# Attention values held stationary, probabilities scaled on ScalarE ahead of their transposes, and a new order of the mixer units

## The reference

```python
u = rmsnorm(x, g_mix)
q, k, v, xb, yb = split(u @ w_in + b_in)
# attention: blocks of 128 queries, each with its own and the previous 128 keys
s = q @ k.T / 8 - slopes * dist                 # masked outside the window
m = max(max(s), sink);  p = exp(s - m)
p = p / (sum(p) + exp(sink - m));  attn = p @ v
# recurrence
xc = causal_conv4(xb)
a = exp(-8 * sigmoid(xc @ w_a) * softplus(-lam))
h[t] = a[t] * h[t-1] + sqrt(1 - a[t]**2) * (sigmoid(xc @ w_i) * xc)[t]
h_res = x + concat(attn, h * gelu(yb)) @ w_out + b_out
y = h_res + (silu(g) * up) @ w_ffn_out          # then a final rmsnorm
```

## Time and profile before

| | |
|---|---|
| time, three runs | 2332.24, 2332.38, 2334.09 us; median 2332.38 |
| span of the profiled execution (first to last instruction) | 2331.0 us |
| TensorE busy | 2251.5 us, 97% |
| VectorE busy | 1302.4 us, 56% |
| ScalarE busy | 878.1 us, 38% |
| granted TensorE clock, mean | 0.985 of full speed |
| bytes from HBM | 196.44 MB, 88 GB/s with the writes |

### The profile page before, as it was taken

How to read it: one execution, slowest core, us unless ns; L and a number is a source line. 1 busy time by engine, 2 the same in 40 slices (tenths; PEclk the granted TensorE clock), 3 DMA queues, 4 the chain that set the end, 5 groups by cost and what they waited for, 6 DMA issues and landing times.

```text
span 2331.0 us, 31209 instructions
## 1 busy us (share of the span) xinstructions
PE 2251.5 (97%) x12165; PEld 1915.8 (82%) x12165; DVE 1302.4 (56%) x2146; ACT 878.1 (38%) x1349; POOL 32.4 (1%) x66
## 2 busy tenths in 40 slices
PE   6999999999999999999999999999999899999996
PEld 6777888888777888888877788888888799999996
DVE  4786535356587544445668653545668665444453
ACT  4574223235375322223457432323446532222221
POOL 1000000000000000000000000000000000000000
PEclk9999999999999999999999999999999899999998
DMA  4123232323313233332322323233231122222221
GB/s 148 55 68 114 91 100 90 101 89 92 101 46 118 91 97 93 92 98 92 107 67 63 119 91 98 91 97 94 92 124 45 30 91 86 87 91 82 92 80 60
DMA packets 58586, 207.34 MB, mean 89 GB/s; under 512 B 7341, under 2 KB 7549, under 8 KB 58416
## 3 DMA queue, kind: packets, MB, share of 16 engines
q1 hardware_dynamic: 51840, 184.57, 25.5%
q0 software_dynamic: 3936, 12.03, 1.5%
q10 hardware_dynamic: 2656, 8.62, 1.0%
HBM read 196.44 MB, written 9.77 MB: 88 GB/s over the span
## 4 chain that ended last, share of the span: by engine, by line
PE 84%; DVE 9%; ACT 4%; issue 2%; DMA 1%; ACTq 0%; DVEq 0%; POOL 0%
PE bank L533 27%; PE bank L535 27%; PE bank L534 27%; DVE s_p L1258 2%; DVE w_lo L1157 1%; DVE xc L1297 1%; PE bank L661 1%; ACT s_p L961 1%; DVE om L1326 1%; PE bank L628 1%; DVE pT L1277 1%; PE bank L583 1%; ACT L986 0%; PE bank L557 0%; DVE ii L1325 0%
## 5 line engine op out<-in xcount | busy, mean ns | idle before, releaser
L533 PE MATMUL bank<-x_hi,w_hi 128*128 128x512 f32 (+1 forms) x2320 | 826.4, 356 | 3.7 <-DVE x_lo L1187 2.6
L535 PE MATMUL bank<-x_hi,w_lo 128*128 128x512 f32 (+1 forms) x2320 | 820.3, 354 | 0.0
L534 PE MATMUL bank<-x_lo,w_hi 128*128 128x512 f32 (+1 forms) x2320 | 819.5, 353 | 0.0
L883 ACT ACTIVATE w_hi<-w_raw 128x1024 fp32r<-128x1024 f32 (+1 forms) x360 | 374.1, 1040 | 1175.3 <-PE bank L535 1175.3
L533 PEld LDWEIGHTS bank<-x_hi,w_hi 128*128 128x128 f32 x2320 | 438.9, 189 | 79.8 <-issue 13.6
L1157 DVE TENSOR_TENSOR w_lo<-w_raw,w_hi 128x1024 fp32r<-128x1024 f32 (+1 forms) x360 | 431.8, 1200 | 127.7 <-ACT w_hi L883 125.9
L534 PEld LDWEIGHTS bank<-x_lo,w_hi 128*128 128x128 f32 x2320 | 439.1, 189 | 61.8 <-issue 1.4
L535 PEld LDWEIGHTS bank<-x_hi,w_lo 128*128 128x128 f32 x2320 | 438.3, 189 | 60.8
L533 PE MATMUL bank<-a_hi,w_hi 128*128 128x512 f32 (+1 forms) x1200 | 427.4, 356 | 6.2 <-DVE a_lo L1561 1.8
L535 PE MATMUL bank<-a_hi,w_lo 128*128 128x512 f32 (+1 forms) x1200 | 425.0, 354 | 0.0
L534 PE MATMUL bank<-a_lo,w_hi 128*128 128x512 f32 (+1 forms) x1200 | 424.3, 354 | 0.0
(11 more groups left out here) (240 smaller groups left out, 1475.0 us busy)
## 6 DMA issues: line engine op xcount, KB each, us to landing
w_raw<-in_units SPq DMA_DIRECT2D x296, 512.0 KB, 3.5
w_raw<-in_units SPq DMA_DIRECT2D x64, 448.0 KB, 3.3
x_tok<-in_x_prompt POOLq DMA_DIRECT2D x16, 512.0 KB, 6.1
out_y_p<-y_tok ACTq DMA_DIRECT2D x16, 512.0 KB, 3.0
gfin<-in_g_fin POOLq DMA_DIRECT2D x1, 512.0 KB, 7.1
kc_tok<-in_cache_k POOLq DMA_DIRECT2D x1, 512.0 KB, 6.9
vc_tok<-in_cache_v POOLq DMA_DIRECT2D x1, 512.0 KB, 7.3
out_nk_s<-in_cache_k POOLq DMA_DIRECT2D x1, 496.0 KB, 6.5
```

Source lines behind the costliest of these rows:

```text
L533: nc.tensor.matmul(out, h, hi[:, kt, c0:c1], start=(first and kt == kts[0]), stop=False)
L534: nc.tensor.matmul(out, h, lo[:, kt, c0:c1], start=False, stop=False)
L535: mm = nc.tensor.matmul(out, l, hi[:, kt, c0:c1], start=False, stop=(kt == kt_of[u] - 1))
L883: w_hi_ready.by(A(w_hi[:, u % RING, 0:n], w_raw[:, u % RAW, 0:n], ACT.Copy))
```

## The change

- `attend` takes the values as the stationary operand (128x64) and the transposed probabilities as the moving one (256 columns: both heads of a group). Group 0 writes partitions 0 to 63 of bank V, group 1 partitions 64 to 127, in turn for each half of the window: 4 matmuls. The result is transposed as it stands; `attn_out`, `attn_T`, `a_tok` and the first copy of `attn_hi` are gone, and `attn_hi` and `attn_lo` read bank V.
- The division by the sum moves ahead of the transposes: `normed`, four ScalarE copies with a scale for each unit, which wait for `rec_ready` from VectorE.
- TensorE's order becomes `scores(s)`, `attend(s-2)`, half of the projection unit, `gates` on odd s, the other half, `probs_T(s-1)`.
- ScalarE's order becomes `exps(s)`, `normed(s-1)`, `lru_root` (even s), `attn_hi` and `lru_gates` (odd s), the bias or the square, the copy of `probs_T(s-1)`, `gelu_tanh`, then as before. VectorE's copy of `probs_T(s-1)` moves behind `evacuate`, and `lru_scan` moves from behind `evacuate` to ahead of it.
- The channels of the attention output now lie in another order, so the 8 units of the output projection are loaded by 5 transfers each (one of half the unit, four of 64 KB) in place of one.

```diff
@@ load_unit (SyncE)
-                raw_in[u % RAW].by(sp.dma_start(w_raw[:, u % RAW, 0:n], units[u % NU, :, 0:n]))
+                raw, src, landed = w_raw[:, u % RAW, :], units[u % NU], raw_in[u % RAW]
+                if u % NU not in U_O:
+                    landed.by(sp.dma_start(raw[:, 0:n], src[:, 0:n]))
+                    return
+                landed.by(sp.dma_start(raw[:, JT * P:n], src[:, JT * P:n]))
+                for g in range(NKV):
+                    for c in range(2):
+                        k = 2 * g + c
+                        landed.by(sp.dma_start(
+                            raw[g * HEAD:(g + 1) * HEAD, 2 * c * P:2 * (c + 1) * P].rearrange("d (o m) -> d o m", o=2),
+                            src[:, k * P:(k + 1) * P].rearrange("(o d) m -> d o m", o=2)))
@@ mixers (TensorE)
 def probs_T(s):
-                    p_ready.wait(pe, b, s + 1)
+                    probs_ready.wait(pe, b, s + 1)
 def attend(s):
-                        attn_moved.wait(pe, b, qb)
-                    for hh in range(HH):
-                        g, jj = hh // 2, hh % 2
-                        head = g * JT + 2 * jp + jj
-                        for half in range(2):
-                            mm = nc.tensor.matmul(V[:, head * HEAD:(head + 1) * HEAD],
-                                                  pT[:, s % 2, 2 * hh + half, :],
-                                                  v_tok[:, qb + half, g * HEAD:(g + 1) * HEAD],
-                                                  start=(half == 0), stop=(half == 1))
+                        amix_ready.wait(pe, b, qb)
+                    for half in range(2):
+                        for g in range(NKV):
+                            d = slice(g * HEAD, (g + 1) * HEAD)
+                            mm = nc.tensor.matmul(V[d, 2 * jp * P:2 * (jp + 1) * P], v_tok[:, qb + half, d],
+                                                  pT[:, s % 2, 4 * g + half:4 * g + half + 3:2, :],
+                                                  start=(half == 0), stop=(half == 1), skip_group_check=True)
-                def attn_T(qb):
-                    atok_ready.wait(pe, b, qb + 1)
-                    for c in range(4):
-                        mm = nc.tensor.transpose(V[:, c * P:(c + 1) * P], a_tok[:, c * P:(c + 1) * P], ident[:, :])
-                    attnT_done.by(mm)
                 for s in range(NUN):
+                    scores(s)
+                    if s >= 2:
+                        attend(s - 2)
+                    if last:
+                        gemm(b, last, UH + s, x_hi, x_lo, None, None, 0)
+                    else:
+                        gemm(b, last, UH + s, x_hi, x_lo, None, list(range(KT // 2)))
+                    if s % 2 == 1:
+                        gates(s // 2)
+                    if last:
+                        gemm(b, last, UH + s, x_hi, x_lo, None, None, 1)
+                    else:
+                        gemm(b, last, UH + s, x_hi, x_lo, None, list(range(KT // 2, KT)))
                     if s >= 1:
                         probs_T(s - 1)
-                    if s >= 2:
-                        attend(s - 2)
-                    scores(s)
-                    gemm(b, last, UH + s, x_hi, x_lo)
-                    if s % 2 == 1:
-                        gates(s // 2)
-                    if s >= 3 and s % 2 == 1:
-                        attn_T((s - 3) // 2)
+                part(0, early)
+                attend(NUN - 2)
                 probs_T(NUN - 1)
-                attend(NUN - 2)
-                part(0, early)
+                part(1, early)
                 attend(NUN - 1)
-                part(1, early)
-                attn_T(QB - 1)
@@ mixers (ScalarE)
                 def attn_hi(qb):
-                    attnT_done.wait(act, b, qb + 1)
-                    attn_moved.by(A(a_tok[:, :], V[:, :], ACT.Copy))
-                    attn_moved.wait(act, b, qb + 1)
-                    amix_hi.by(A(a_hi[...], a_tok[...], ACT.Copy))
+                    av_done.wait(act, b, 2 * qb + 2)
+                    amix_hi.by(A(a_hi[...], V[...], ACT.Copy))
+                def normed(s):
+                    rec_ready.wait(act, b, s + 1)
+                    for hh in range(HH):
+                        head = hh // 2 * JT + 2 * (s % 2) + hh % 2
+                        ins = A(s_p[:, s % 2, hh, :], s_p[:, s % 2, hh, :], ACT.Copy,
+                                scale=rec[:, s // 2 % 2, head:head + 1])
+                    probs_ready.by(ins)
                 for s in range(NUN):
+                    exps(s)
                     if s >= 1:
-                        probs_T(s - 1)
-                    exps(s)
+                        normed(s - 1)
                     if s >= 2 and s % 2 == 0:
                         lru_root((s - 2) // 2)
+                    if s >= 3 and s % 2 == 1:
+                        attn_hi((s - 3) // 2)
+                    if s % 2 == 1:
+                        lru_gates(s // 2)
                    ...
-                        if c < LC - 1:
-                            gelu_tanh(c)
-                    if s >= 3 and s % 2 == 1:
-                        attn_hi((s - 3) // 2)
-                    if s % 2 == 1:
-                        lru_gates(s // 2)
+                    if s >= 1:
+                        probs_T(s - 1)
+                    if kind == "y" and c < LC - 1:
+                        gelu_tanh(c)
+                normed(NUN - 1)
                 probs_T(NUN - 1)
@@ mixers (VectorE)
                 for s in range(NUN):
-                    if s >= 1:
-                        probs_T(s - 1)
                     softmax_1(s)
                    ...
-                    if s >= 3 and s % 2 == 1:
-                        attn_out((s - 3) // 2)
                    ...
+                    if s >= 2 and s % 2 == 0:
+                        lru_scan((s - 2) // 2)
                    ...
+                    if s >= 1:
+                        probs_T(s - 1)
                    ...
-                    if s == NUN - 1:
-                        probs_T(s)
-                    if s >= 2 and s % 2 == 0:
-                        lru_scan((s - 2) // 2)
                     if kind == "y":
                         gelu_arg(c)
                 softmax_2(NUN - 1)
+                probs_T(NUN - 1)
```

More of the change, by code:

```diff
@@ L195, in hymba_layer @@
         h_prev = place("h_prev", [P, LC])
-        a_tok = place("a_tok", [P, NH * HEAD], at=[top[0]])
         ssum = place("ssum", [P, W])
@@ L282, in sem @@
             return ctx.enter_context(nc.semaphore(name))
-        raw_in = [Signal(sem(f"raw_in{i}"), NU // RAW, 16) for i in range(RAW)]
+        transfers = [1 + NKV * 2 if u in U_O else 1 for u in range(NU)]
+        raw_count = [sum(transfers[u % RAW:u + 1:RAW]) for u in range(NU)]
+        raw_in = [Signal(sem(f"raw_in{i}"), sum(transfers[i::RAW]), 16) for i in range(RAW)]
         w_hi_ready = Signal(sem("w_hi_ready"), NU)
@@ L320, in hymba_layer @@
         av_done = Signal(sem("av_done"), NUN)
-        atok_ready = Signal(sem("atok_ready"), QB)
-        attnT_done = Signal(sem("attnT_done"), QB)
-        attn_moved = Signal(sem("attn_moved"), QB)
+        rec_ready = Signal(sem("rec_ready"), NUN)
+        probs_ready = Signal(sem("probs_ready"), NUN)
         amix_hi = Signal(sem("amix_hi"), QB)
@@ L492, in _ @@
             for s in (gemm_done, xT_done, statx_done, stath_done, staty_done, vT_done, sc_done, pT_done,
-                      av_done, attnT_done,
+                      av_done,
                       gates_done, yT_done):
@@ L500, in smp_by, with gemm @@
                 ins.then_inc(smp_pe, 1)
[L502 to L508, removed]
+            def gemm(b, wide, u, hi, lo, tile_ready=None, kts=None, only=None, begins=0):
+                kts = kts or list(range(kt_of[u]))
+                first = kts[0] == begins
                 final = kts[-1] == kt_of[u] - 1
@@ L703, in part @@
                 def part(m, kts, c=0):
-                    gemm(b, last, U_O[m], a_hi, a_lo, mix_ready, kts, c)
+                    gemm(b, last, U_O[m], a_hi, a_lo, mix_ready, kts, c, KT - LC if kts else 0)
                 early, late, end_ = list(range(KT - LC, KT - 2)), [KT - 2] + list(range(KT - LC)), [KT - 1]
+                part(0, early)
+                attend(NUN - 2)
                 probs_T(NUN - 1)
-                attend(NUN - 2)
-                part(0, early)
+                part(1, early)
                 attend(NUN - 1)
-                part(1, early)
-                attn_T(QB - 1)
                 ahead = 2 if last else 3
@@ L860, in _ @@
             for s in (w_hi_ready, z_ready, sqx_ready, sqh_ready, sqy_ready, xhi_ready, hhi_ready, stdx_ready,
-                      stdh_ready, stdy_ready, p_ready, pTa_ready, attn_moved, amix_hi,
+                      stdh_ready, stdy_ready, p_ready, pTa_ready, probs_ready, amix_hi,
```

(24 more changed lines are left out.)

3 lines of the change are left out of this document (1 added, 2 removed).

## The result

The changed kernel takes 2419.45 us (median of 4 runs, 2415.77 to 2420.97) against 2332.31 for the kernel before: ratio 1.037, 95% interval 1.0355 to 1.0384. It is slower by 87 us; forecast was 2404, range 2368 to 2426.

A forecast was written before the change was run, and what follows sets the result against it. The prediction took the order of steps on three nearly full engines, a loop mostly through VectorE, as the bound. Blocks +59.6 and clock +12 made 72 on the 2331.0 span: 2403, 2404 us as time, range 2368 to 2426.

The forecast's parts named there:

- The loop: Durations added along the engines' new written orders for a steady mixer pair: 26.16 us against 23.04, 3.1 more per pair.
- 26 to 27.5 named as a sign of being right: Length in us of a steady pair that the changed profile would show if the forecast held.
- the first pair: First mixer pair of a block, from scores(1), added up to 23.6 us; two pairs of 26.16 follow.
- the tail: Stretch of a block from scores(7) on, 62.54 us before: forecast to grow by 6.7.
- ahead of scores(1): Start of a block, where unit 0's transposes move behind product 1: -0.9 us.
- The clock: TensorE's clock falling after empty waits: 1 us at three waits per block, bounds 0 and 2, +12 us in all.
- The last block: Wider products and sample steps between, yet taken to grow like the other blocks: 14.9 us, bounds 8 and 22.
- Attend: The two groups' `attend` products run side by side on TensorE: 0.93 us with the start, bounds 0.86 and 1.8.
- the rival with turns: The two groups take turns in TensorE, `attend` stays at 1.8 us: +10 in all, 2414; chance 0.20.
- Transfers at 0: Output-projection units in five pieces: a split 1.5 to 6 us late is hidden, cost taken as 0.
- TensorE alone as the bound: Rival: root and scan don't hold up the evacuation, pairs fall by TensorE's shed work: -35 us, 2298; chance 0.08.
- Loss and gain that cancel: Rival: the orders let slip about half of the wait and the clock holds: 2332 within a few us; chance 0.05.

The follow-up runs named there:

- Experiment 1: Changed kernel with VectorE's scan put back behind the evacuation and the pT copy: 2385.6 us.
- experiment 4: Changed kernel with unread products filling TensorE's waits, 16 ahead of `attend` on odd s, 8 ahead of the transposes on even s, in the three loop blocks: 2403.1 us.
- experiment 3: Changed kernel with `normed` cut to one copy of one column, so the attention output isn't divided by its sum: 2399.5 us.
- Experiment 11: Changed kernel with scan back, early scaling, `attend` between product halves, gates behind the product, and the last block's sample steps moved on TensorE, VectorE and ScalarE: 2329.4 us.
- 8: Changed kernel with scan behind the evacuation, scaling of unit s-1 early, `attend` between the product's halves and gates behind the whole unit: 2340.2 us.
- experiment 6: Changed kernel with output-projection rows packed beforehand so each unit arrives as one 512 KB transfer: 2421.5 us.

## Why the prediction was right, and where its sizes were off

**Direction and mechanism: right.** VectorE idles 2.4 us ahead of the scan for the root (forecast 2.5). TensorE waits at `attend` for ScalarE's pT copy, 2.4 to 4.1 us (forecast 4), and 2 to 3 us at the transposes for `normed` (forecast 2 to 3). Experiment 1 takes the first away by one move and 34 us with it, so it is shown as a cause and not only as a place.

**The loop: right.** 26.16 was added up; the steady pairs are 26.26 and 26.09 with TensorE's waits filled (experiment 4). In the changed kernel they are 29.53 and 26.75, at clocks of 0.79 and 0.91, so one of the two lies outside the 26 to 27.5 named as a sign of being right. The rest of the block, again with the waits filled, in block 2: the first pair 25.1 (forecast 23.6), the tail +4.7 (forecast +6.7), ahead of scores(1) +0.5 (forecast -0.9). Together +15.7 against a forecast of +14.9; that these three misses nearly cancel is luck. In block 1 they are 25.3, +6.3 and -0.8, together +16.3: there the tail and the start are near the forecast, and the first pair alone is 1.7 too long. Why it is stays open.

**The clock: term too small.** 12 us were put down for four blocks. The three blocks of the loop alone give back 3.0, 6.0 and 6.9, 15.9 in all, when the waits are filled. In block 2 the clock is low in five stretches behind the first, 27 us together, and before in one of 3.4. The term is thus 6 to 7 us in blocks 1 and 2, at the upper bound of 2 us for each of three waits or above it, and not the 3 taken; 5.1 and 5.4 of it lie in the three pairs and 1.6 in each tail.

Which wait lowers the clock is another matter. In the second pair of block 2 it falls at 1256.9, behind the 1.89 us wait at the transposes and ahead of the longer one at `attend`, and stays low to 1267.2. Two lines of the changed kernel and, below them, `attend` of the second pair of experiment 1:

```profile
1255.62 1.09 PE L655 MATMUL bank<-ident,s_p 128*128 128x128 f32 x8 [1.89 <-ACT s_p L1014]
1261.92 1.97 PE L673 MATMUL bank<-pT,v_tok 128*64 128x256 f32 x8 [3.45 <-ACT pT L976]
```

```profile
1236.88 1.92 PE L673 MATMUL bank<-pT,v_tok 128*64 128x256 f32 x8 [0.20 <-ACT pT L976]
```

`attend` takes 1.08 us at full clock. In experiment 1 it is as slow as here, 1.92, though it waits only 0.20: there only the 1.89 us wait at the transposes stands ahead of it. In experiment 3, where that wait is 0.4 to 0.7 us, `scores` runs at full clock (1.14), and `attend` behind its wait of 4.0 to 4.1 at the low one (1.97 and 1.98). The Trainium skill (TensorE: Matmul & The Clock Gate, HAM oscillation) said that TensorE, waiting between bursts, starts the next one at half rate. The traces agree with that, behind waits of 1.9 us and of 4.

**The last block: term too small.** It was taken to grow like the others, 14.9 (bounds 8 and 22), and 3 for the clock; it grew by 26.9. The step that failed is "I take the same for it". Nor does it look like the same cause: the scan's place, worth 10 to 12 us in a block of the loop, gives nothing back here (experiment 1, 202.0 against 199.6, at clocks of 0.85 and 0.87), and leaving out the scaling gives 7.4 (experiment 3). Its sample steps now stand directly behind the transposes, whose banks must be copied out first:

```profile
1898.93 1.86 PE L794 MATMUL bank<-pcT,vc_tok 128*64 128x16 f32 x16 [5.93 <-ACT pT L976]
```

```profile
1903.87 0.97 DVE L1486 COPY mixs<-bank 64x32 f32<-64x32 f32 x8 [5.69 <-PE bank L796]
```

The clock is low from 1895 to 1916 there. Experiment 11 moves these steps, on top of 8, and gets 10.6 us back. What makes the rest of the last block's growth stays open.

**The sum.** Blocks of the loop +64.1 (forecast 53.7 with the clock), last block +26.9 (17.9), everything else -2.7: +88.3 on the span, 72 forecast.

**Attend: right.** Side by side, 0.1 us a record, 1.08 us for the eight where 0.93 was taken; TensorE's work in a pair falls by 1.7 us (kernel 11) where 2.1 to 2.3 was forecast; the rival with turns (+10) was worth 9.4 and did not come. The Trainium skill (TensorEngine Tiling (Array Packing), Key Properties) says that a change of tiling mode drains TensorE. No wait over 0.1 us shows between `scores` and `attend` at full clock; the first record of `attend` is 0.05 us longer (0.43 against 0.38).

**Transfers at 0: right** (experiment 6: 2 us, within the spread of the runs).

**The other rivals.** TensorE alone as the bound does not hold for the change. With the same arithmetic in another order (8 and 11) the pair comes within 1.5 us of TensorE's work, but the time stays 31 us above that rival's 2298 (kernel 11), for the tails and the last block take their part. Loss and gain that cancel is what kernel 11 shows, not the change.

## What to carry to other kernels

When an edit brings new operands and a new order in one step, judge them apart: here the new operands shed 1.7 us of TensorE's work a pair, and the order lost it and 3 us more. Walk each engine's written order as one loop with rows of the trace as terms; it came within 0.1 us of the pair, while the last block, taken "as in the other blocks", and the clock, taken as a round number, were off by 9 and 7 us. A wait can hide the next one behind it: a move that removes the first may cost more than it gains until the second is moved too.

## What the runs showed that I had not expected

- The clock fell again inside pairs in which TensorE is 80% busy, at waits of 2 to 4 us with short work around them. The loss is larger than the waits' number suggests: filling them with 72 unread products a block gave 3.0, 6.0 and 6.9 us back. In experiment 1 the clock fell behind waits of 1.9 and 2.2 us with only transposes and `scores` after them.
- Two kernels with equal waits at the same place can part there: the sample scores took 2.13 us in one and 3.02 in the other, and 10 us of low clock followed in the second alone.
- Two 64-column products in different column halves take 0.10 us a record, the same in one half 0.23, while each record's own duration reads 0.38 in both: a record's duration doesn't tell the overlap, the starts do.
